# Turning activation chunks with VectorE block transposes and on-chip transfers instead of TensorE transposes

## The reference

```
hn = rms_norm(h, g0); proj = hn @ w_in           # gMLP: 3*4096 columns
y  = u * (ws_causal @ v + b) * silu(zg);  h += y @ w_out
hn = rms_norm(h, g1); q,k,v,zg = hn @ w_in       # stick-breaking attention, 16 heads
h += (attention(q,k,v) * silu(zg)) @ w_out;  h = rms_norm(h, final_g)
xn = rmsnorm(h);  proj = xn @ w_in_2             # mLSTM (4 heads), softmax attention (8 heads), gates
h_m, h_a = mlstm(...) , attention(...)
merged = sigmoid(g_m) * (h_m @ w_branch_m) + sigmoid(g_a) * (h_a @ w_branch_a)
x = x + rmsnorm(merged @ w_out_2)
x = x + rmsnorm(square(relu(rmsnorm(x) @ w_up)) @ w_down)
```

## Time and profile before

| | |
|---|---|
| time, median of 3 runs | 2688.58 us (2687.36 to 2688.68) |
| span of the profiled execution | 2687.2 us |
| mean granted TensorE clock | 0.994 |
| TensorE busy, matmuls | 98% |
| VectorE busy / ScalarE busy | 58% / 46% |
| DMA engines, mean rate | 183 GB/s |

### The profile page before, as it was taken

How to read it: one execution, slowest core, us unless ns; L and a number is a source line. 1 busy time by engine, 2 the same in 40 slices (tenths; PEclk the granted TensorE clock), 3 DMA queues, 4 the chain that set the end, 5 groups by cost and what they waited for, 6 DMA issues and landing times.

```text
span 2687.2 us, 30213 instructions
## 1 busy us (share of the span) xinstructions
PE 2646.0 (98%) x12077; PEld 2190.0 (81%) x12077; DVE 1548.1 (58%) x1822; ACT 1227.4 (46%) x1513; POOL 25.9 (1%) x49
## 2 busy tenths in 40 slices
PE   7999999999999999999999999999999999999997
PEld 6888888888888888888888888888778888888886
DVE  4545555555556666666866665555565555554555
ACT  5544443444444444455444444444454344443443
POOL 1000000000000000000000000000000000000000
PEclk9999999999999999999999999999999999999999
DMA  6666656665565555555555655665655665655653
GB/s 208 209 195 188 194 183 192 190 194 184 181 188 173 169 169 166 186 195 187 169 174 155 190 170 175 192 189 188 200 156 187 194 184 192 188 186 193 187 191 121
DMA packets 254987, 492.31 MB, mean 183 GB/s; under 512 B 15472, under 2 KB 17632, under 8 KB 254848
## 3 DMA queue, kind: packets, MB, share of 16 engines
q1 hardware_dynamic: 251376, 481.37, 57.8%
q0 software_dynamic: 2384, 6.93, 1.0%
q10 hardware_dynamic: 1088, 2.10, 0.2%
HBM read 488.24 MB, written 2.10 MB: 182 GB/s over the span
## 4 chain that ended last, share of the span: by engine, by line
PE 97%; DVE 1%; ACT 1%; DMA 1%; issue 0%; SPq 0%; DVEq 0%; ACTq 0%
PE bank L33 94%; PE bank L36 3%; DMA t_stage<-in_a_w_in_dram 1%; ACT t_junk L39 0%; DVE t_hres L51 0%; DVE t_wl L48 0%; ACT t_wh L39 0%; SPq L69 0%; DVE t_pool L48 0%; ACT t_xth L39 0%; DVE t_rq L51 0%; DVE t_rq L48 0%; DVE t_scl L51 0%; DVE t_xtl L51 0%; ACT t_vreg L39 0%
## 5 line engine op out<-in xcount | busy, mean ns | idle before, releaser
L48 DVE TENSOR_TENSOR t_wl<-t_stage,t_wh 128x1024 fp32r<-128x1024 f32 x920 | 1114.0, 1216 | 877.2 <-ACT t_wh L39 868.1
L39 ACT ACTIVATE t_wh<-t_stage 128x1024 fp32r<-128x1024 f32 x920 | 963.3, 1052 | 895.9 <-PE bank L33 878.2
L33 PE MATMUL bank<-t_wl,t_xth 128*128 128x512 f32 x2496 | 993.7, 398 | 11.7 <-DVE t_xtl L51 7.9
L33 PE MATMUL bank<-t_wh,t_xtl 128*128 128x512 f32 x2496 | 975.8, 391 | 0.0
L33 PE MATMUL bank<-t_wh,t_xth 128*128 128x512 f32 x2496 | 974.5, 390 | 0.0
L33 PEld LDWEIGHTS bank<-t_wl,t_xth 128*128 128x128 f32 x2496 | 470.4, 188 | 105.6 <-DVE t_xtl L51 8.1
L33 PEld LDWEIGHTS bank<-t_wh,t_xtl 128*128 128x128 f32 x2496 | 469.9, 188 | 100.8
L33 PEld LDWEIGHTS bank<-t_wh,t_xth 128*128 128x128 f32 x2496 | 470.7, 189 | 93.6 <-issue 0.2
L33 PE MATMUL bank<-t_wl,t_yth 128*128 128x512 f32 x1024 | 401.7, 392 | 0.0
L33 PE MATMUL bank<-t_wh,t_ytl 128*128 128x512 f32 x1024 | 398.9, 390 | 0.0
L33 PE MATMUL bank<-t_wh,t_yth 128*128 128x512 f32 x1024 | 398.5, 389 | 0.0
(11 more groups left out here) (178 smaller groups left out, 964.4 us busy)
## 6 DMA issues: line engine op xcount, KB each, us to landing
t_stage<-in_a_w_in_dram SPq DMA_DIRECT2D x192, 512.0 KB, 3.9
t_stage<-in_w_in_dram SPq DMA_DIRECT2D x176, 512.0 KB, 3.8
t_stage<-in_b_w_in_dram SPq DMA_DIRECT2D x128, 512.0 KB, 3.7
t_stage<-in_w_up_dram SPq DMA_DIRECT2D x128, 512.0 KB, 3.7
t_stage<-in_w_down_dram SPq DMA_DIRECT2D x128, 512.0 KB, 3.6
t_stage<-in_a_w_out_dram SPq DMA_DIRECT2D x64, 512.0 KB, 4.0
t_stage<-in_b_w_out_dram SPq DMA_DIRECT2D x32, 512.0 KB, 4.1
t_stage<-in_w_out_dram SPq DMA_DIRECT2D x32, 512.0 KB, 3.8
```

What stands on the lines that cost most here:

```text
L33: return lambda e: e.matmul(*a, **k)
L39: return lambda e: e.activation(*a, **k)
L48: return lambda e: e.tensor_tensor(*a, **k)
```

## The change

Forty-four of the 52 chunks are turned in a new way; `to_xt_now` keeps the old one for the 4 chunks of x and the 4 before the feed-forward. The new `to_xt` hands out two pieces. `send` takes a temporary and makes two VectorE transposes of 128 x 512 (`STREAM_TRANSPOSE`), which turn each 32 x 32 block in its place; then SP issues four transfers from SBUF to SBUF, one for each 32 partitions, 128 KB each in runs of 1 KB, into the low tensor. `divide`, at least two groups later, waits for them, makes the high part from it on ScalarE and the rest in place on VectorE, 1024 columns each (with a gain: four of each, of 256 columns). The source is released after the VectorE transposes.

A chunk of a turned tensor now lies as (token, kt mod 4, half), with `[128, 4, 1024]` for the whole. The stationary operand of every large product, 128 tokens of one half and one kt, is read with a step of 8 elements (32 bytes), and so is the streaming operand of `proj_gates`; `to_xt_now` and the pieces with a gain write with that step. A VectorE transpose reads with a step of 4 elements and writes with one of 8.

```diff
-    xth, _ = sb("xth", [128, 16, S], F32R)
-    xtl, _ = sb("xtl", [128, 16, S], F32R)
-    yth, yt_at = sb("yth", [128, 16, S], F32R)
-    ytl, _ = sb("ytl", [128, 16, S], F32R)
+    xth, _ = sb("xth", [128, 4, 1024], F32R)
+    xtl, _ = sb("xtl", [128, 4, 1024], F32R)
+    yth, yt_at = sb("yth", [128, 4, 1024], F32R)
+    ytl, _ = sb("ytl", [128, 4, 1024], F32R)
...
+    mth, _ = sb("mth", [128, 4, 1024], F32R, offset=v_at)
+    mtl, _ = sb("mtl", [128, 4, 1024], F32R, offset=v_at + 16384)
...
+    s_turn = [sem(f"turn{i}") for i in range(4)]
...
+    def turned_chunk(x, c):
+
+        return x[:, c, :].rearrange("p (t k i) -> p t k i", k=4, i=2)
+
+    def tokens(x, kt, i):
+
+        return turned_chunk(x, kt // 4)[:, :, kt % 4, i]
+
+    def all_tokens(x, kt):
+
+        return turned_chunk(x, kt // 4)[:, :, kt % 4].rearrange("p t i -> p i t")
...
-                    h, l = xh[:, kt, 128 * i:128 * i + 128], xl[:, kt, 128 * i:128 * i + 128]
+                    h, l = tokens(xh, kt, i), tokens(xl, kt, i)
...
-                PE.run(lambda e: e.matmul(o, w_l, xh[:, k, :], start=(k == 0), stop=False))
-                PE.run(lambda e: e.matmul(o, w_h, xh[:, k, :], start=False, stop=False))
-                mark = PE.do(lambda e: e.matmul(o, w_h, xl[:, k, :], start=False, stop=(k == 15)))
+                PE.run(lambda e: e.matmul(o, w_l, all_tokens(xh, k), start=(k == 0), stop=False))
+                PE.run(lambda e: e.matmul(o, w_h, all_tokens(xh, k), start=False, stop=False))
+                mark = PE.do(lambda e: e.matmul(o, w_h, all_tokens(xl, k), start=False, stop=(k == 15)))
...
-    def to_xt(src, marks, c, xh, xl, ready, gain=None, scale=1.0, done=None, wait=1):
+    def to_xt_now(src, marks, c, xh, xl, ready, gain):
...
-                if gain is None:
-                    tv = t.rearrange("p (k s) -> p k s", k=2)
-                    a = AC.do(lambda e: e.activation(xh[:, k:k + 2, :], tv, ACT.Copy, scale=scale), tp)
-                    v = DV.do(lambda e: e.scalar_tensor_tensor(
-                        out=xl[:, k:k + 2, :], in0=tv, scalar=scale, in1=xh[:, k:k + 2, :].bitcast(F32),
-                        op0=ALU.mult, op1=ALU.subtract), a)
-                else:
-                    gain_mark = m_par.get("gc", m_g0)
-                    for kk in range(2):
-                        a = AC.do(lambda e, kk=kk: e.activation(xh[:, k + kk, :], t[:, 256 * kk:256 * kk + 256],
-                                                                ACT.Copy, scale=gain[:, k + kk:k + kk + 1]),
-                                  tp, gain_mark)
-                    for kk in range(2):
-                        v = DV.do(lambda e, kk=kk: e.scalar_tensor_tensor(
-                            out=xl[:, k + kk, :], in0=t[:, 256 * kk:256 * kk + 256],
-                            scalar=gain[:, k + kk:k + kk + 1], in1=xh[:, k + kk, :].bitcast(F32),
-                            op0=ALU.mult, op1=ALU.subtract), a, gain_mark)
+                gain_mark = m_par.get("gc", m_g0)
+                tv = [t[:, 256 * kk:256 * kk + 256].rearrange("p (i t) -> p i t", i=2) for kk in range(2)]
+                for kk in range(2):
+                    a = AC.do(lambda e, kk=kk: e.activation(all_tokens(xh, k + kk), tv[kk], ACT.Copy,
+                                                            scale=gain[:, k + kk:k + kk + 1]), tp, gain_mark)
+                for kk in range(2):
+                    v = DV.do(lambda e, kk=kk: e.scalar_tensor_tensor(
+                        out=all_tokens(xl, k + kk), in0=tv[kk], scalar=gain[:, k + kk:k + kk + 1],
+                        in1=all_tokens(xh, k + kk).bitcast(F32), op0=ALU.mult, op1=ALU.subtract), a, gain_mark)
                 trans.give(n, v)
                 ready[k] = ready[k + 1] = (v,)
-                if b == 1 and done is not None:
-                    done(tp)
-            later((piece, wait if b == 0 else 1))
+            later(piece)
+
+    turn_count = [0]
+
+    def to_xt(src, marks, c, xh, xl, ready, gain=None, scale=1.0, done=None, wait=1):
+
+        st = {}
+
+        def send():
+            zn, z, free = temps.take()
+            zv = z.rearrange("p x y -> p (x y)")
+            blocks = zv.rearrange("p (b s k i) -> p b k i s", b=4, k=4, i=2)
+            for i in range(2):
+                turned = DV.do(lambda e, i=i: e.block_transpose(
+                    blocks[:, :, :, i], src(i).rearrange("p (k r b) -> p b k r", k=4, b=4)), *marks, *free)
+            if done is not None:
+                done(turned)
+            n = turn_count[0]
+            turn_count[0] += 1
+            s_ = s_turn[n % 4]
+            before = ((s_, 64 * (n // 4)),) if n >= 4 else ()
+            for a in range(4):
+                landed = SP.dma(lambda e, a=a: e.dma_start(
+                    xl[:, c, 256 * a:256 * a + 256].bitcast(F32), zv[32 * a:32 * a + 32, :]),
+                    s_, 64 * (n // 4) + 64, turned, *before)
+            temps.give(zn, landed)
+            st["landed"] = landed
+
+        def divide():
+            raw, hi, lo = xl[:, c, :].bitcast(F32), xh[:, c, :], xl[:, c, :]
+            if gain is None:
+                a = AC.do(lambda e: e.activation(hi, raw, ACT.Copy, scale=scale), st["landed"])
+                v = DV.do(lambda e: e.scalar_tensor_tensor(out=lo, in0=raw, scalar=scale, in1=hi.bitcast(F32),
+                                                           op0=ALU.mult, op1=ALU.subtract), a, st["landed"])
+            else:
+                gain_mark = m_par.get("gc", m_g0)
+                for k in range(4 * c, 4 * c + 4):
+                    a = AC.do(lambda e, k=k: e.activation(all_tokens(xh, k), all_tokens(xl, k).bitcast(F32), ACT.Copy,
+                                                          scale=gain[:, k:k + 1]), st["landed"], gain_mark)
+                for k in range(4 * c, 4 * c + 4):
+                    v = DV.do(lambda e, k=k: e.scalar_tensor_tensor(
+                        out=all_tokens(xl, k), in0=all_tokens(xl, k).bitcast(F32), scalar=gain[:, k:k + 1],
+                        in1=all_tokens(xh, k).bitcast(F32), op0=ALU.mult, op1=ALU.subtract),
+                        a, st["landed"], gain_mark)
+            for k in range(4 * c, 4 * c + 4):
+                ready[k] = (v,)
+        later((send, wait), (divide, 2))
...
-        to_xt(lambda i, c=c: hres[:, i, cols(c)], (x_in[c],), c, xth, xtl, x_ready, gain=gc[:, 0:16])
+        to_xt_now(lambda i, c=c: hres[:, i, cols(c)], (x_in[c],), c, xth, xtl, x_ready, gc[:, 0:16])
...
-        to_xt(lambda i: hres[:, i, cols(c)], X3Mark(c), c, xth, xtl, x_ready, gain=gc[:, 64:80])
+        to_xt_now(lambda i: hres[:, i, cols(c)], X3Mark(c), c, xth, xtl, x_ready, gc[:, 64:80])
```

More of the change, by code:

```diff
@@ L36, in transpose, with block_transpose @@
         return lambda e: e.transpose(*a, **k)
+    def block_transpose(self, out, in_):
+        return lambda e: e.transpose(out, in_)
     def activation(self, *a, **k):
@@ L201, in _program @@
     vreg, v_at = sb("vreg", [128, 8192])
-    mth, _ = sb("mth", [128, 16, S], F32R, offset=v_at)
-    mtl, _ = sb("mtl", [128, 16, S], F32R, offset=v_at + 16384)
+    mth, _ = sb("mth", [128, 4, 1024], F32R, offset=v_at)
+    mtl, _ = sb("mtl", [128, 4, 1024], F32R, offset=v_at + 16384)
     pool4, _ = sb("pool4", [128, 4, 2, 512])
```

## The result

The changed kernel takes **2856.7 us** (median; 2856.1 to 2857.0, 4 runs). The kernel before takes 2688.2 us on the same chip. The ratio is **1.063 [1.061, 1.064]**: 6.3% slower, where 1.3% faster was forecast. The time lies outside the range given.

A forecast was written before the change was run, and what follows sets the result against it. TensorE's matmuls, busy 98% of the span, were taken as the bound. 2687.2 - 43.3 + 0 + 2.9 + 2.4 + 2.0 = 2651.2 us of span, with 1.4 for the median of runs about 2653 us; range 2644 to 2714.

The forecast's parts named there:

- I take 0: Wide matmuls: loading the stationary operand with a step of 8 stays hidden under 0.227 us of streaming, adding 0 us.
- the hidden case: The main forecast, with the strided load still hidden under the wide matmul: likeliest 2644 to 2665 us, chance 0.66.
- Rival (a): Wide matmuls: the strided load comes out of its cover by a little, +57 us, 2710 us; chance 0.10.
- (b): Wide matmuls: load exceeds its cover by a lot, 3265 us at a factor of 2.5, 3881 at triple; chance 0.15.
- The upper end given for small misses: Whole kernel: the sum with upper ends of gates and steps and a landing of 6 us, 2662 us.
- What was removed: TensorE: 88 pieces of four transposes, 39.3 us, and delays before twenty pieces, 4.0 us; together -43.3 us.
- The gates: Gate product, 48 matmuls streaming 256 tokens with the step: 0 to +5.8 us, middle +2.9 taken.
- VectorE's transposes: Two block transposes of 128 x 512 per chunk, 691 ns each, hidden beside matmuls, costing nothing by themselves.
- Landing: On-chip transfers of a turned chunk: 3.7 us until landed, ends 2.3 and 10.8.
- The late chunk: Chunk 3 of `yth`, second attention, divided right before its reader: TensorE waits 2.4 us once, ends 1.1 and 14.7.
- (c): Late chunks: turning and landing 4 us longer gives 2660 us, far ends 2738; chance 0.07.
- Strided writes: Chunks kept on TensorE, at x and before the feed-forward: copies 0.21 us longer each, 0 to 4 us, +2.0 taken.

The follow-up runs named there:

- e1: Kernel before, every transpose kept on TensorE, only the turned tensors laid out so the stationary operand has a step of 8: 2901.5 us, ratio 1.079.
- e5: Changed kernel, but transfers land in a separate tile and the dividing copies write tokens side by side, no step in the stationary operand: 2676.1 us, ratio 0.996.
- e11: Separate program, not the kernel: lines of 96 matmuls, other engines idle, streamed columns varied at stationary steps 1, 2, 4, 8; 247 ns at step 8, 512 columns.
- e8: Separate program, not the kernel: lines of 96 matmuls, other engines idle, stationary step varied from 1 to 64; 227 ns at step 1, 247 at 8, 512 columns.

## Why the prediction was wrong

**The step that failed is "I take 0" for the stationary operand.** The method held: the load alone is 0.113 us, measured again as at most 0.1125, the cover is 0.227, and the load may slow down by a factor of 2.0. The factor at step 8 is at least 2.15, so the term put at 0 was 17.4 ns a matmul, +190.4 us. The text saw that cover and doubled load are equal to a nanosecond and still gave the hidden case 0.66. With a price unknown by a factor of more than two and a term of 10.9 us for each nanosecond, nothing in the rows supported that chance.

**Rival (a) was what happened**, at 0.10, and was priced too low. It took a load of 0.226 plus half of the fixed 13 ns, 232 ns and 2710 us; with all of it, 239 and 2786. The load itself is 0.242, so no fixed part had to be argued, and the distance is 244; the 2 ns between them belong to what stays open. Its decisive point, a load slowed by 2.04, was passed. (b) is refuted: no step measured takes a factor of 2.5 (step 12, the dearest, needs 271 ns).

The upper end given for small misses, 2662, is 2 us more than its own terms make (2687.2 - 43.3 + 5.8 + 4.7 + 4.0 + 1.4 = 2660); nothing hangs on it.

**The rule cited from the Trainium skill**, page "SBUF — State Buffer" (door 1), spoke against the change, and the result agrees as far as step 8 goes. Its sentence on two hits in a line of 16 bytes sorts the loads rightly: at step 2, with two tokens in a line, a load takes at most 0.120 us, at 4, 8 and 32, with one, 0.226 to 0.242. Its sentence that a float32 step of up to 4 is free does not hold here: a step of 4 takes 0.235 us, and even step 2 costs the kernel 72 us. The measurement decides.

**What was removed**, -43.3: right. From e1 to the changed kernel it is -44.7; there a piece costs 0.55 us, 88 make 48.5, and the waits of 2.2 and 2.1 us give 4.3 of it back.

**The gates**: +2.9 taken, upper end +5.8, measured +4.8. The wait of 2.1 us for `t_wl` ahead of them was not forecast. That the step also lengthens the 66 pieces that stay (+6.9) was left out, because with a hidden load there is nothing to lengthen.

**VectorE's transposes**: 0.69 us taken, 1.215 measured, well inside the bounds of 0.43 and 3.35. The Trainium skill's "VectorE: DVE Perf Modes" (the three transpose paths) has 311 ns for 128 x 128 in bf16; four times that is 1.24, an estimate, and the trace agrees. It should have been the value taken. **Landing**: 3.7 taken, from one load of 512 KB; measured 4.7 at the tight place and 4.8 in the median. One transfer takes 2.7; what was missed is that four are issued one after another. **The late chunk**: 2.4 us, once; measured 2.2, once. That the number fits is luck, since the chunk was 1.7 us later than forecast and TensorE 1.9 us later at it. With no wait at the ten other places and 1.7 us more and not 4, (c) did not come in this kernel. Late chunks did come in e5, at two places, where the copies are twice as long. **Strided writes**: VectorE's copy of 256 columns at x takes 705 ns (479 in e5, where the tokens lie side by side), near the 0.21 us more that was taken; the waits for `t_xtl` at x and before the feed-forward are 7.1 + 1.7 us and were 7.9 + 1.0, so the +2.0 did not come.

## What to carry to other kernels

A weight load that is hidden has a margin, and the margin can be worked out: streaming time less the load alone. Before an operand's layout is changed, hold that margin against the worst plausible factor, and where they meet within a few per cent call it a coin toss, not zero. If data has to arrive with its elements apart, let a copy that runs anyway on an idle engine put them side by side, and cut that copy small, because each engine serves its instructions in order and a long copy holds up the splits behind it. A few short waits of TensorE cost more than their length when its granted clock falls after them.

## What the runs showed of the hardware

- A stationary operand of 128 float32r columns takes at most 0.1125 us to load side by side, at most 0.120 with a step of 2, 0.235 with 4, 0.242 with 8 and 0.226 with 32 (192 columns streamed over it for the first two, 256 for the others). The order is not that of the step. It was not expected that 32 is cheaper than 8, or that with 512 columns steps of 12 (271 ns) and 24 (255 ns) are dearer than 16 and 64 (239 and 237).
- The streamed operand takes double with a step: 454 ns for 512 columns at step 2, 461 at step 4, for 227.
- TensorE's reads with a step of 8 do not follow the clock. At a granted clock of 0.50, that is 1.2 GHz, the load took 214 ns side by side (e11, 128 columns) and 239 ns at step 8 (e8, 64 columns); at 1.00 (2.4 GHz) it takes at most 112.5 and 242. The streamed operand is alike: in the changed kernel the gate matmuls, streaming with a step of 8, are 0.218 us apart at a granted clock of 0.50 (1330 to 1333 us) and at 1.00 (1334 to 1338 us).
- VectorE's block transpose of 128 x 512 float32 took 1.215 us, reads with a step of 8 doubled VectorE's and ScalarE's copies (1.23 to 2.17 and 1.06 to 2.14 us for 1024 columns), and an on-chip transfer of 128 KB in runs of 1 KB landed in 2.7 us; four, issued one after another, took 4.8 us from the first issue to the last landing (medians).
